# Modulation rows of a two-layer diffusion backbone made by TensorE in column quarters, with every loop written out

## The reference, cut to what matters

```python
def adaln(cond, w, b):
    m = jax.nn.silu(cond) @ w + b            # w: 2048 x 6144
    return jnp.split(m, 3, axis=-1)
...
    shift, scale, gate = adaln(c, ada_w[i], ada_b[i])
    shift_c, scale_c, gate_c = adaln(c_ctx, ada_w[i], ada_b[i])
    h = rmsnorm(x, norm_w[i]) * (1.0 + scale[:, None]) + shift[:, None]
    hc = rmsnorm(ctx, norm_w[i]) * (1.0 + scale_c) + shift_c
    # layer 0: gated linear attention, 4 heads; layer 1: differential softmax attention, 8 heads
    x = x + gate[:, None] * y
```

## Time and profile before

| | us |
|---|---|
| median of 3 runs | 2059.52 (2059.32 to 2062.37) |
| profiled execution, its own time | 2059.49 |
| its span on the core | 2057.7 |
| PE busy | 1778.6 (86% of the span) |
| DVE busy | 1362.7 (66%) |
| POOL, ACT busy | 731.9, 636.9 |
| mean granted TensorE clock | 0.911 of full |

### The profile page before, as it was taken

One profiled execution on the slowest core, in us unless ns is written; L12 is line 12 of the kernel. 1 busy time (PEld: TensorE's weight loads), 2 busy tenths in 40 slices (PEclk: granted clock), 3 DMA queues, 4 the chain that ended last, 5 costly groups with the idle time before them and its releaser, 6 DMA issues.

```text
span 2057.7 us, 23754 instructions
## 1 busy us (share of the span) xinstructions
PE 1778.6 (86%) x7612; PEld 1354.8 (66%) x7612; DVE 1362.7 (66%) x1891; ACT 636.9 (31%) x853; POOL 731.9 (36%) x296
## 2 busy tenths in 40 slices
PE   5787988988898889888698996899999999999598
PEld 1225777667676776676376875687777777777366
DVE  4667698578757885788587776837557466375541
ACT  2002432242224223422232224334334334343232
POOL 0003243223322332242034331635455355355065
PEclk8788999989898989898899998999999999999799
DMA  8675334343434343434245661423233233233144
GB/s 283 225 237 166 111 94 138 119 149 102 130 115 147 116 129 111 150 108 132 79 131 166 187 198 42 150 75 118 82 116 118 71 122 122 71 122 103 31 152 133
DMA packets 188997, 265.04 MB, mean 129 GB/s; under 512 B 19530, under 2 KB 103428, under 8 KB 188420
## 3 DMA queue, kind: packets, MB, share of 16 engines
q1 hardware_dynamic: 184100, 256.70, 39.7%
q10 hardware_dynamic: 4832, 7.60, 1.2%
HBM read 262.14 MB, written 2.10 MB: 128 GB/s over the span
## 4 chain that ended last, share of the span: by engine, by line
PE 34%; DVE 31%; issue 21%; DMA 11%; ACT 1%; DVEq 1%; SPq 0%; POOL 0%; ACTq 0%; POOLq 0%
PE bank L680 22%; DMA ada_w<-in_ada_w 11%; DVE u L992 6%; PE bank L813 2%; DVE work L1288 2%; PE bank L764 2%; PE bank L649 2%; PE bank L905 1%; DVE work L992 1%; DVE work L1117 1%; PE bank L889 1%; DVE work L1330 1%; PE bank L760 1%; DVE acts_lo L1076 1%; DVE work L1168 1%
## 5 line engine op out<-in xcount | busy, mean ns | idle before, releaser
L414 POOL TENSOR_TENSOR w_lo<-w_raw,w_hi 128x1024 fp32r<-128x1024 f32 x288 | 730.1, 2546 | 1311.8 <-ACT w_hi L426 1311.1
L680 PE MATMUL bank<-w_lo,acts_hi 128*128 128x512 f32 x1664 | 672.6, 404 | 55.3 <-DVE work L1341 26.7
L680 PE MATMUL bank<-w_hi,acts_hi 128*128 128x512 f32 x1664 | 658.4, 396 | 0.0
L680 PE MATMUL bank<-w_hi,acts_lo 128*128 128x512 f32 x1664 | 657.7, 395 | 0.0
L426 ACT ACTIVATE w_hi<-w_raw 128x1024 fp32r<-128x1024 f32 x288 | 301.9, 1057 | 756.0 <-PE bank L680 557.2
L680 PEld LDWEIGHTS bank<-w_lo,acts_hi 128*128 128x128 f32 x1664 | 319.1, 192 | 143.1 <-issue 53.2
L992 DVE SCALAR_TENSOR_TENSOR u<-ada_w,silu_c,u 128x512 f32<-128x512 f32 x360 | 327.4, 960 | 84.8 <-DMA ada_w<-in_ada_w 83.8
L680 PEld LDWEIGHTS bank<-w_hi,acts_lo 128*128 128x128 f32 x1664 | 318.7, 192 | 68.7
L680 PEld LDWEIGHTS bank<-w_hi,acts_hi 128*128 128x128 f32 x1664 | 319.1, 192 | 65.7 <-issue 1.7
L992 DVE SCALAR_TENSOR_TENSOR work<-ada_w,silu_c,work 128x512 f32<-128x512 f32 x120 | 119.2, 1045 | 42.7 <-DMA ada_w<-in_ada_w 42.7
L680 PE MATMUL bank<-acts_hi,w_lo 128*128 128x512 f32 x256 | 102.4, 400 | 14.2 <-DVE acts_lo L1076 14.2
(11 more groups left out here) (160 smaller groups left out, 1773.9 us busy)
## 6 DMA issues: line engine op xcount, KB each, us to landing
ada_w<-in_ada_w SPq DMA_DIRECT2D x256, 256.0 KB, 2.9
w_raw<-in_diff_w_in SPq DMA_DIRECT2D x256, 256.0 KB, 2.8
w_raw<-in_gla_w_in SPq DMA_DIRECT2D x192, 256.0 KB, 3.4
w_raw<-in_ada_w SPq DMA_DIRECT2D x64, 512.0 KB, 5.0
w_raw<-in_gla_w_out SPq DMA_DIRECT2D x64, 256.0 KB, 3.8
w_raw<-in_diff_w_out SPq DMA_DIRECT2D x64, 256.0 KB, 3.4
u<-in_x SPq DMA_DIRECT2D x2, 1024.0 KB, 9.1
u<-in_ctx SPq DMA_DIRECT2D x2, 1024.0 KB, 13.1
```

The costliest lines, as they stand in the source:

```text
L414: pool.tensor_tensor(w_lo[:, p % RING], raw[:, p % RING], w_hi[:, p % RING].bitcast(F32), ALU.subtract).then_inc(w_split, 1)
L680: last = pe.matmul(bank[t][:], a, b, start=(k == 0 and i == 0), stop=(k == NK - 1 and i == 2))
```

## The change

- The modulation is made by TensorE alone. The two SiLU columns stand in a stationary tile of 32 columns, 30 of them zero (`silu_p`). A quad is four k-tiles, loaded by one 1 MB transfer; its four matmuls write the four 32-partition quarters of one bank, `b[32j:32j+32]`, each with 512 moving columns. Four quads make a chunk. ScalarE copies the bank to `ada_rows` (128 x 512), and four matmuls with a 0/1 matrix `sel` of two columns add the quarters and bring the rows to columns.
- In the start 32 quads go through four slots of 1 MB (two in a larger `ada_w`, two in `raw`).
- The 16 background chunks are 64 quads through two slots, at pairs given by `quad_after`: two chunks in each GLA head, one in each of the four `OUT0` chunks, and four in attention heads 0, 2, 4 and 6. The sum comes one pair after the last quad.
- VectorE's `weigh`, `startup_tiles` and `background_tiles` are gone.
- `unit_scores` 0 comes after pair 6 instead of 5, and waits for `ada_taken`. The wait for `d2_ok` moves to the next head's start.
- All `Fori` loops are written out. ScalarE presets a table set that holds Ln and Exp after each SiLU.

```diff
+def quad_after(m):
+    i, q = m // 4, m % 4
+    if i < 2 * G_HEADS:
+        return (3 * (i // 2) + i % 2) * PAIRS + ((0, 1, 3, 4) if i % 2 else (0, 1, 3, 5))[q]
+    if i < 2 * G_HEADS + 4:
+        return (OUT0 + i - 2 * G_HEADS) * PAIRS + (0, 1, 3, 5)[q]
+    return (DIFF + 4 * (i - 2 * G_HEADS - 4)) * PAIRS + (5, 7, PAIRS + 2, PAIRS + 5)[q]
...
+            def startup_quad(n):
+                if n >= 4:
+                    sp.wait_ge(ada_used, n - 3)
+                a, q = n // 4, n % 4
+                sp.dma_start(quad_slot[n % 4], aw0[:, 4 * q:4 * q + 4, a * CW:(a + 1) * CW]).then_inc(ada_in[n % 4], 16)
...
-                    if ada_from is not None:
-                        for k in (2 * p, 2 * p + 1):
-                            sp.wait_ge(ada_used, c * NK + (k + 1))
-                            sp.dma_start(ada_w[:, k % 2], ada_from[0][:, k, bass.ds(ada_from[1], CW)])\
-                                .then_inc(ada_in[k % 2], 16)
+                    for m in range(4 * BACKGROUND):
+                        if c * PAIRS + p == (quad_after(m - 2) + 5 if m >= 2 else 0):
+                            background_quad(m)
...
+            def log_and_exp():
+                act.preload_act_table_set("natural_log_exp_and_others")
...
+            def modulation_rows(a):
+                b = bank[6 + a % 2] if a < STARTUP else bank[7]
+                act.wait_ge(ada_used, 4 * a + 4)
+                if a > 0:
                     act.wait_ge(mod_sum, a)
+                act.activation(ada_rows[:], b[:], ACT.Copy).then_inc(row_ok, 1)
...
+            def ada_quad(n, slot, b):
+                q = n % 4
+                pe.wait_ge(ada_in[slot], 16 * (n // 4 + 1) if n < QUADS else 16 * (STARTUP + (n - QUADS) // 2 + 1))
+                if q == 0 and n >= 8:
+                    pe.wait_ge(ada_taken, n // 4 - 1 if n < QUADS else n // 4)
+                for j in range(4):
+                    last = pe.matmul(b[32 * j:32 * j + 32, :], silu_p[:, 4 * q + j, :], quad_slot[slot][:, j, :],
+                                     start=(q == 0), stop=(q == 3), skip_group_check=True)
+                last.then_inc(ada_used, 1)
+
+            def modulation_sum(a, b):
+                pe.wait_ge(row_ok, a + 1)
                 for n in range(4):
-                    for m in range(2):
-                        last = pe.matmul(b[:, 2 * n + m:2 * n + m + 1], acc[:, m, n * P:(n + 1) * P],
-                                         ones[:, 0:1], start=(n == 0 and m == 0), stop=last_part,
-                                         skip_group_check=True)
+                    last = pe.matmul(b[:, 2 * n:2 * n + 2], ada_rows[:, n * P:(n + 1) * P], sel[:],
+                                     start=(n == 0), stop=True, skip_group_check=True)
+                last.then_inc(mod_sum, 1)
...
                 pe.wait_ge(til_ok, h * 4 + (n + 1))
+                if n == 0:
+                    pe.wait_ge(ada_taken, STARTUP + 2 * h + 2)
...
                 c = h * 3
+                if h > 0:
+                    pe.wait_ge(d2_ok, h)
                 project(c, lambda t: c, False, before=before)
-                background(c, mod_acc_g)
                 if gates is not None:
                     gates()
                 gate_logits(h)
                 project(c + 1, lambda t: c + 1, True,
-                        after=lambda p: unit_scores(h, 0) if p == 5 else None)
+                        after=lambda p: unit_scores(h, 0) if p == 6 else None)
 
                 def after(p):
-                    if p == 3:
-                        pe.wait_ge(d2_ok, h + 1)
-                        background(c + 1, mod_acc_v)
                     if p in (0, 3, 6):
                         unit_scores(h, {0: 1, 3: 2, 6: 3}[p])
 
                 project(c + 2, lambda t: c + 2, True, after=after)
-                background(c + 2, mod_acc_g)
                 head_outputs(h)
...
-                st.step(last)
-                st.wait()
-                unit_tildes(h, 0, (c + 1, mod_acc_v, range(6, 9)))
-                background_tiles(c + 1, mod_acc_v, range(9, 11))
-                unit_tildes(h, 1, (c + 1, mod_acc_v, range(11, 13)))
+                unit_tildes(h, 0)
+                take_modulation(STARTUP + 2 * h + 1, 3, h * 4)
+                unit_tildes(h, 1)
 
                 for t in range(NT):
                     complete(h * 9 + 3, c + 1, t)
                     dve.tensor_copy(v_sb[:, t], bank[t][:]).then_inc(freed[t], 1)
-                background_tiles(c + 1, mod_acc_v, range(13, NK))
-                background_tiles(c + 2, mod_acc_g, range(0, 2))
-                unit_tildes(h, 2, (c + 2, mod_acc_g, range(2, 5)))
+                unit_tildes(h, 2)
```

More of the change, by code:

```diff
@@ L197, in build @@
         raw_in = [sem(f"raw_in{i}") for i in range(RING)]
-        ada_in = [sem(f"ada_in{i}") for i in range(2)]
+        ada_in = [sem(f"ada_in{i}") for i in range(4)]
         xres_in = sem("xres_in")
@@ L409, in _ @@
             pool.memset(a2[:], 0.0).then_inc(const_in, 1)
-            with pool.Fori(0, CHUNKS) as c:
+            pool.memset(silu_p[:, :, 2:32], 0.0).then_inc(const_in, 1)
+            for c in range(0, CHUNKS):
                 for p in range(PAIRS):
@@ L568, in _ @@
             for j in range(1, 4):
-                splits(j + OUT0, range(4))
+                splits(j + OUT0, range(2))
+                modulation_rows(STARTUP + 2 * G_HEADS + j - 1)
+                splits(j + OUT0, range(2, 4))
                 load_residual(j)
@@ L620, in _ @@
             attention_head(0, False)
-            with act.Fori(1, A_HEADS) as h:
-                st.enter(h - 1, 3)
+            for h in range(1, A_HEADS):
                 attention_head(h, True)
-                st.leave(A_HEADS - 1)
             softmax(A_HEADS - 1)
@@ L633, in store @@
                     act.dma_start(out[0][t * P:(t + 1) * P, bass.ds(j * CW, CW)], yrow[:, t]).then_inc(y_out, 16)
-            with act.Fori(1, 4) as j:
+            for j in range(1, 4):
                 splits(j + OUT1, range(4))
@@ L713, in _ @@
             pe.wait_ge(silu_ok, 2)
[L715 to L737 removed]
+            for n in range(QUADS):
+                ada_quad(n, n % 4, bank[6 + n // 4 % 2])
+                if n % 4 == 0 and n > 0:
+                    modulation_sum(n // 4 - 1, bank[6 + (n // 4 - 1) % 2])
+            modulation_sum(STARTUP - 1, bank[6 + (STARTUP - 1) % 2])
             def gate_columns():
@@ L840, in _ @@
             gla_head(0, before=transposing(0, xn), gates=gate_columns)
-            with pe.Fori(1, G_HEADS) as h:
+            for h in range(1, G_HEADS):
                 gla_head(h)
@@ L856, in _ @@
             project(OUT0, lambda t: OUT0, True, before=transposing(1, u))
-            background(OUT0, mod_acc)
-            with pe.Fori(OUT0 + 1, DIFF) as c:
+            for c in range(OUT0 + 1, DIFF):
                 project(c, lambda t: c, True)
-                background(c, mod_acc)
             def frees(h, second):
@@ L917, in _ @@
             attention_head(0, before=transposing(2, xn))
-            with pe.Fori(1, A_HEADS) as h:
+            for h in range(1, A_HEADS):
                 attention_head(h, behind={0: key_transposes, 1: query_transposes, 2: attention_scores,
@@ L927, in _ @@
             project(OUT1, lambda t: OUT1, True, tiles=2, before=transposing(3, u1, 2))
-            with pe.Fori(OUT1 + 1, CHUNKS) as c:
+            for c in range(OUT1 + 1, CHUNKS):
                 project(c, lambda t: c, True, tiles=2)
@@ L1070, in weighted, with activation_tiles @@
                 return emit
[L1072 removed]
+            def activation_tiles(stage, buf, emit, width=TOK):
                 def low(k):
@@ L1135, in gla_head @@
                 c = h * 3
-                if not first:
-                    background_tiles(c, mod_acc_g, range(NK))
+                take_modulation(STARTUP + 2 * h, 2, h * 4)
                 for t in range(NT):
@@ L1393, in _ @@
             queries(0)
-            with dve.Fori(1, A_HEADS) as h:
-                st.enter(h - 1, 33)
+            for h in range(1, A_HEADS):
                 attend(h - 1)
@@ L1417, in _ @@
             result(0, True)
-            with dve.Fori(1, 4) as j:
+            for j in range(1, 4):
                 result(j, False)
```

253 lines of the change are left out of this document (92 added, 161 removed).

## The result

The changed kernel takes 1943.87 us (median of 4 runs, 1939.34 to 1947.20) against 2060.19 us for the kernel before on the same chip: a ratio of 0.943, with a 95% interval of 0.9415 to 0.9451. The time lies in the predicted range (1874 to 1965), 41 us above the predicted 1903, and outside the 1880 to 1930 that the prediction gave its own mechanism. The profiled execution took 1944.98 us, its span is 1942.9 us.

A forecast was written before the change was run, and what follows sets the result against it. It took the start to be bound by slot hand-back and GLA heads to wait for late VectorE; -61.2 - 70.7 - 1.3 + 4.2 - 7.0 - 16.7 - 3.8 = -156.5 from 2059.49 gave 1903 us, range 1874 to 1965.

The forecast's parts named there:

- its own mechanism: Whole kernel: the prediction's main case, quads of 1.3 us and a transfer-bound start, 1903 us, range 1880 to 1930, chance 69%.
- halved streams: Quads, a rival: the four streams halve each other, a quad costs 2.2 us, 1961 us in all; chance 13%.
- the last quad at 119: Start: transfers at 355 GB/s are the bound, 29.4 MB take 83 us; saved 35.7 us.
- The quad's price: Four matmuls in four column quarters: 1.3 us, of it 0.86 for the streams and 0.4 for two tiling changes.
- the stall: GLA heads, start of chunk c+2: TensorE waits 6.2 us for VectorE's copies of v, plus 2 at half clock.
- so neither makes a wait: GLA heads 1 to 3: VectorE's unit 2 and 3 tildes have 16 us for a chain of 11.
- big transfers in the way of small ones: SP's queue, a rival: a weight pair waits behind 1 MB (3 us), 24 us more, 1927 us; chance 8%.
- +4.2: `OUT0`: 16 quads (20.8 us) and 4 sums (4.2) bring the stage from 208.8 to 213 us.
- -16.7: Attention: odd heads 76.5 us, even heads 81.4, head 0 +0.5, in sum 16.7 us saved.
- an odd head loses 1.3 of waiting at its second chunk, 2.2 of the 3 before the next head and 1.7 of half clock: Attention: two table loads of 1.28 us fewer in VectorE's chain shorten an odd head to 76.5 us.
- Tables: ScalarE's table loads saved: 1.3 us in the gate rows, two loads of 1.28 per attention head, 3.8 in the tail.
- Loops at 0: Whole kernel: written-out loops priced at 0, between -5 us (branches gone) and +10 us (code to be loaded).

The follow-up runs named there:

- e6: The changed kernel with each quad of the start loaded by two transfers of 512 KB instead of one of 1 MB: 1944.15 us, ratio 0.9435.
- e10: e2 with a GLA head's quads and units spread wider, plus the edits of e7 and e8: 1849.93 us, ratio 0.896.
- e1: The changed kernel with a quad's four matmuls all writing the same column quarter, so one behind the other: 2080.23 us, ratio 1.008.
- e4: e2 with unit 0's scores after pair 5 again and the second modulation's quads after pairs 0 to 3: 1893.73 us, ratio 0.918.
- e2: The changed kernel with SP issuing each background quad's load one pair earlier: 1921.46 us, ratio 0.930.
- e8: e4 with VectorE making a chunk's four products in `OUT0` before its four residual additions: 1882.12 us, ratio 0.912.
- e11: The changed kernel with GpSimd's subtraction cut to 32 of 512 columns after the first four pairs, leaving out computation: 1853.66 us, ratio 0.8985.
- e7: e4 with VectorE copying queries and gate out of their banks before the last addition of the keys' rotation: 1883.16 us, ratio 0.914.
- e3: The changed kernel without the preset of the common table for Ln and Exp: 1987.67 us, ratio 0.963.
- e5: The kernel before with all its loops written out and nothing else changed: 2058.20 us against 2059.69, ratio 0.9995.

## Why the prediction was right, and where it was off by 41 us

The mechanism was right: the thin products cost TensorE little when they stand side by side, the start became bound by its transfers, and VectorE's old waits went. That the time lies in the range is in part luck: it is 14 us outside the 1880 to 1930 of the prediction's own mechanism, and the upper end of 1965 came from halved streams that did not happen. And waits that were not foreseen were partly paid for by work that was priced too dear.

**The start: right, and better than said.** The prediction took transfers at 355 GB/s as the bound and the last quad at 119; it was 111.5, at 366 GB/s. e6 shows that the size of the transfers is not the reason; the hand-back of slots is what SP's waits before point to, together with the greater depth. The gain was then lost again behind it: the first projection came at 127.3, 15.8 us after the last quad, of which 9.5 are a wait for VectorE's first activation tiles. That wait isn't in the prediction's 7 us from the last quad to the first split weights; head 0 ended 3.4 us late.

**The quad's price: right.** Predicted 1.3 us with bounds 1.0 and 3.7. Three quads of e10's head 1:
```profile
323.07 1.07 PE L678 MATMUL bank<-ada_w,silu_p 128*32 128x512 f32 x8
...
335.18 1.06 PE L678 MATMUL bank<-ada_w,silu_p 128*32 128x512 f32 x8
...
341.84 1.06 PE L678 MATMUL bank<-ada_w,silu_p 128*32 128x512 f32 x8
```
Two pairs and a quad take 12.11 us, one pair and a quad 6.66: a pair is 5.45 and a quad 1.21. (From its start to the next projection record it takes only 0.99, but the record before it and the one behind it each take some 0.1 us longer than the 0.23 of the others.) In e1 the same sum gives 364.02 - 354.81 - 5.45 = 3.76, three times as much. With 0.86 for four streams side by side, 0.35 are left for both changes of tiling, and with 3.4 for the streams one behind the other, again some 0.35 in e1: close to the 0.4 that the prediction had taken. The Trainium skill ("TensorEngine Tiling (Array Packing)", Key Properties) says that a change of tiling mode drains TensorE; these 0.35 us a quad are all that it can cost here. What was too dear is the rest of a head: a unit takes 2.6 us instead of 2.85, and by e10's timeline the logits 3.7 instead of 4.9 and the head outputs 9.9 instead of 11.5. Together with the quads a head is some 5 us cheaper than predicted: 179.6 - 8.2 for the stall would be 171.4, and e10's head without waits is 166.6.

**GLA heads: 184 instead of 180.** The stall came where the prediction said, at c+2, and e4 removes it. Its size was 8.24 us of waiting and 2.2 of lower clock (7.7 us for 24 records instead of 5.5), against 6.2 + 2: the chain from unit 0's scores to the end of the first copy took 13.9 us, not 11.65, since two of its products took 2.83 us each, where the chain before had one slow product (2.62). The step that failed is the DMA one: *"so neither makes a wait"* was argued for VectorE, and the quads' loads were costed only as a rival ("big transfers in the way of small ones", 8%). The reverse happened: the small ones' waits stood in front of the big load on SP. It cost 2.6 to 4.2 us in heads 1 to 3, with the lower clock behind it; e2 gets 22 us back. The sum is 166.6 for the work, 10.4 for the stall and some 7 for the late load: only because the work was 5 us cheaper a head does 184 look close to 180.

**`OUT0`: +11.4 instead of +4.2.** The prediction counted quads and sums (1.3 and 1.05 a piece) and left out that the old sum at the chunk's end had covered the hand-back of the last bank. With the sum moved into the chunk three waits of 2.4 us appear, each with a lower clock behind it; e8 takes them away. They cost 14 us, so without them the stage would have come out some 7 us below the forecast: its chunks, too, were priced too dear (49.4 us in e8, 51.3 by the prediction).

**Attention: +2.2 instead of -16.7.** This is the largest miss. Some 5 of the 19 us lie in head 0: one of its quads waits 5.0 us for its load, and the head takes 88.8 us to its queries' copy instead of 83.0, where the prediction had +0.5. The rest lies in the odd heads, which take some 79.8 us instead of 76.5; even heads take 81, as predicted. The step that failed was "an odd head loses 1.3 of waiting at its second chunk, 2.2 of the 3 before the next head and 1.7 of half clock". (These three add to 5.2, so 75.9; the 76.5 is a slip of 0.6.) Two table loads of 1.28 us can't save 3.5 us of waiting: TensorE's 1.3 us at the second chunk bring it 1.3 us earlier to the next wait, and the prediction counted them there again.

And only one of the two loads shortened VectorE's chain. It runs from the copy of the last attention output through the keys to the queries' copy, first before, then after:
```profile
1467.82 0.69 DVE L1383 COPY work<-bank 128x512 f32<-128x512 f32 x1 [8.09 <-PE bank L905]
...
1476.18 1.71 DVE L1311 TENSOR_TENSOR work<-work 128x1024 f32<-128x1024 f32 x1
...
1498.87 1.28 DVE L1341 COPY work<-bank 128x512 f32<-128x512 f32 x2
```
```profile
1437.60 0.69 DVE L1335 COPY work<-bank 128x512 f32<-128x512 f32 x1 [8.06 <-PE bank L921]
...
1444.55 3.18 DVE L1261 TENSOR_TENSOR work<-work 128x1024 f32<-128x1024 f32 x1
...
1467.42 1.27 DVE L1293 COPY work<-bank 128x512 f32<-128x512 f32 x2
```
The chain is 29.8 us instead of 31.05. The first load's 1.3 us are saved; the second's are lost again in the squares of the keys, 3.18 us instead of 1.71, in all seven heads alike. They come earlier now and start 0.3 us after one of GpSimd's subtractions of 2.40 us (1444.25), not 1.8 us after it (1474.41) as before. In e11 the squares take 1.23 us, the chain 26.7, and a head without quads 75.0 us. So the wait for the queries' copy is there by the order of VectorE's program, as e7 shows (6 us), and it did not shrink because of the collision with GpSimd.

**Tables: the place was wrong.** The prediction priced them by the loads next to TensorE's waits: 18 us in the odd attention heads, some 8 in the gate rows, the turn and the tail. They are worth 44 us in the changed kernel (e3), 31 of the profiled 36 in the GLA heads with the gate rows, where the prediction had costed them at 1.3. They were inside the heads' forecast only because this was built from TensorE's own work.

**Loops at 0: right**, by e5, within 0.2% and on the kernel before; in the changed kernel they were not tried alone.

## What to carry to other kernels

Four fp32 matmuls with 32 stationary columns each cost little more than one when they stand in different column quarters (1.21 us against 0.86 for the two records of one): for thin products that VectorE does by weighing it is worth a trial, if the loads keep up. When a stage's own work shrinks, price its neighbours in program order: a load that waits behind another load's semaphore, a bank that was freed under the step that moved, a copy behind an addition. And count a removed wait once: follow the engine to its next wait, and ask whether the chain that ends there has got shorter.

## What the runs showed of the hardware that I had not expected

- VectorE instructions with two SBUF inputs took 0.69 us alone and 2.7 to 2.9 us beside GpSimd's subtraction; in the whole kernel 244 of 836 us of VectorE's busy time go when the subtraction is shortened (e11).
- The shorter waits cost clock too. After a wait of 2.37 us in `OUT0` (in e4, whose `OUT0` is the changed kernel's) some six projection records started 0.43 us apart, the pace of 1.2 GHz, before the spacing was 0.23 again; in the changed kernel the stretch from 440 to 450 us, about the end of the 8.24 us wait, has a granted clock of 0.58.
- The Trainium skill ("DMA: Bandwidth & Descriptors", Specifications) puts a core's share of HBM at about 358 GB/s. The start ran at 366 to 368 GB/s for 80 us, with transfers of 1 MB and of 512 KB alike; where the two differ, the measured rate is the one to use.
